# A decoder step on one core: the last down-projection tile by column halves, the final norm and outputs in two parts

## The reference

```
u = rmsnorm(h, mlp_norm[l]) @ w_up[l]             # 1024 -> 4096
h = h + square(relu(u)) @ w_down[l]               # 4096 -> 1024
...
y = rmsnorm(h, final_norm)                        # h * rsqrt(mean(h*h) + eps) * final_norm
```

## Time and profile before

| | |
|---|---|
| median of three runs | 1713.85 us (1711.11 to 1716.33) |
| the profiled execution | 1711.88 us, its span 1710.1 us |
| TensorE matmuls busy | 1603.4 us, 94% of the span |
| VectorE busy | 833.6 us, 49% |
| ScalarE busy | 562.3 us, 33% |
| DMA | 149.41 MB, mean 87 GB/s |

### The profile page before, as it was taken

How to read it: one execution, slowest core, us unless ns; L and a number is a source line. 1 busy time by engine, 2 the same in 40 slices (tenths; PEclk the granted TensorE clock), 3 DMA queues, 4 the chain that set the end, 5 groups by cost and what they waited for, 6 DMA issues and landing times.

```text
span 1710.1 us, 29033 instructions
## 1 busy us (share of the span) xinstructions
PE 1603.4 (94%) x11509; PEld 1481.6 (87%) x11509; DVE 833.6 (49%) x1227; ACT 562.3 (33%) x879; POOL 79.5 (5%) x93
## 2 busy tenths in 40 slices
PE   3889999878999999999989689999999999999998
PEld 3778999768999999999988456776799999999998
DVE  5845566654542433334576645655454334243343
ACT  4412222333331322323342115554333223132243
POOL 1720000001000000000000000000000000000000
PEclk8899999979999999999999889999999999999999
DMA  6433322203223222222233221543132322222221
GB/s 194 147 122 89 91 87 76 76 27 105 75 87 87 74 86 86 86 74 86 75 90 101 61 79 41 147 133 97 50 87 75 87 74 86 85 74 86 75 85 55
DMA packets 228795, 149.41 MB, mean 87 GB/s; under 512 B 11057, under 2 KB 222402, under 8 KB 228706
## 3 DMA queue, kind: packets, MB, share of 16 engines
q1 hardware_dynamic: 218802, 123.75, 25.2%
q0 software_dynamic: 6112, 20.54, 3.9%
q10 hardware_dynamic: 3792, 3.93, 0.7%
HBM read 140.52 MB, written 7.68 MB: 87 GB/s over the span
## 4 chain that ended last, share of the span: by engine, by line
PE 83%; DVE 11%; ACT 3%; issue 1%; DMA 1%; DVEq 0%; ACTq 0%; SPq 0%
PE ps L576 63%; PE ps L1050 3%; PE ps L1008 2%; DVE wl L1512 2%; PE ps L1077 2%; PE ps L991 1%; PE ps L918 1%; DVE ml L1516 1%; PE ps L953 1%; PE ps L954 1%; PE ps L704 1%; DVE ss L1522 1%; DVE t L1806 1%; PE ps L781 1%; ACT wh L1155 1%
## 5 line engine op out<-in xcount | busy, mean ns | idle before, releaser
L576 PE MATMUL ps<-xh,wh 128*128 128x288 f32 x1542 | 338.7, 302 | 2.2 <-DVE wl L1512 2.2
L576 PE MATMUL ps<-mh,wh 128*128 128x288 f32 (+1 forms) x1424 | 318.4, 300 | 17.9 <-DVE wl L1512 16.6
L576 PE MATMUL ps<-xh,wl 128*128 128x288 f32 x1542 | 331.6, 297 | 0.0
L576 PE MATMUL ps<-xl,wh 128*128 128x288 f32 x1542 | 331.5, 297 | 0.0
L576 PE MATMUL ps<-ml,wh 128*128 128x288 f32 (+1 forms) x1424 | 316.0, 298 | 0.0
L576 PE MATMUL ps<-mh,wl 128*128 128x288 f32 (+1 forms) x1424 | 315.9, 298 | 0.0
L1155 ACT ACTIVATE wh<-raw 128x1024 fp32r<-128x1024 f32 (+1 forms) x195 | 202.2, 1037 | 280.0 <-PE ps L576 262.1
L1512 DVE TENSOR_TENSOR wl<-raw,wh 128x1024 fp32r<-128x1024 f32 (+1 forms) x195 | 236.1, 1211 | 90.1 <-ACT wh L1155 88.7
L576 PEld LDWEIGHTS ps<-xh,wh 128*128 128x128 f32 x1542 | 250.6, 190 | 9.7 <-issue 5.3
L576 PEld LDWEIGHTS ps<-mh,wh 128*128 128x128 f32 x1424 | 236.8, 192 | 20.7 <-DVE wl L1512 17.2
L576 PEld LDWEIGHTS ps<-xl,wh 128*128 128x128 f32 x1542 | 250.1, 190 | 0.0
(11 more groups left out here) (296 smaller groups left out, 1440.9 us busy)
## 6 DMA issues: line engine op xcount, KB each, us to landing
raw<-in_w_up SPq DMA_DIRECT2D x64, 512.0 KB, 4.0
raw<-in_w_down SPq DMA_DIRECT2D x64, 512.0 KB, 3.6
pages<-in_cache_mla SPq DMA_DIRECT2D x128, 160.0 KB, 2.2
raw<-in_a_w_in SPq DMA_DIRECT2D x26, 512.0 KB, 4.0
memkc<-in_cache_mem_k POOLq DMA_DIRECT2D x16, 256.0 KB, 3.9
memvc<-in_cache_mem_v POOLq DMA_DIRECT2D x16, 256.0 KB, 4.5
raw<-in_a_w_out SPq DMA_DIRECT2D x8, 512.0 KB, 4.2
raw<-in_b_w_out SPq DMA_DIRECT2D x8, 512.0 KB, 4.7
```

What stands on the lines that cost most here:

```text
L576: last = mm(ps[:, 2 * (m % 2) + c, 0:n], w[:, s, kk, :], x(kk, col, n), start=(kk == 0 and nth == 0), stop=(kk == k - 1 and nth == 2))
```

## The change

The last down tile of each group is computed as two calls of `dense`, column half 0 first, half 1 behind it. Half 0 now counts on a new semaphore `left_ready`. For tile 194 alone the work behind it is done by halves too: VectorE adds 288 columns of the residual (`y_res`), ScalarE squares them (`y_sq`) and writes 288 columns of `ytmp`, VectorE adds 288 columns to `ss` (`y_ss`), first for half 0, then for half 1. This tile no longer counts on `acc_free` and `sq_used`.

The end runs in two parts: row blocks 0 and 1 (rows 0 to 255, within column half 0), then row blocks 2, 3 and the sample block. In each part come the sums, the roots, the reciprocals, the transposes and the scaled copies. The transposes use banks (n+4)%7 in place of n%7. Each row block leaves in two DMAs of 2 KB rows: SP sends features 0 to 511 when VectorE has them, and ScalarE itself issues the DMA for features 512 to 1023 behind its own copy.

```diff
+        left_ready, y_res, y_sq, y_ss, y_out_act = sem("left_ready"), sem("y_res"), sem("y_sq"), sem("y_ss"), sem("y_out_act")
...
                 sp.wait_ge(y_row_dve, n + 1)
-                sp.wait_ge(y_row_act, n + 1)
                 dst = o["y_p"][0, P * n:P * n + P, :] if n < RT else o["y_s"].rearrange("b t d -> (b t) d")
-                sp.dma_start(dst, yrow[n][0:P if n < RT else NS, :]).then_inc(y_out, 16)
+                sp.dma_start(dst[:, 0:512], yrow[n][0:P if n < RT else NS, 0:512]).then_inc(y_out, 16)
             sp.wait_ge(y_out, 16 * (RT + 1))
+            sp.wait_ge(y_out_act, 16 * (RT + 1))
...
-                if k - 1 in part and half != 0:
-                    last.then_inc(acc_ready, 1)
+                if k - 1 in part:
+                    last.then_inc(left_ready if half == 0 else acc_ready, 1)
...
-                    for j in range(KD):
+                    for j in range(KD - 1):
                         dense(m0 + base + GROUP + j, tiles(mh), tiles(ml), i=i, k=KD,
                               ready=(h_lo, lambda kk: at(h0 + base // 2 + kk + 1, i, GROUP)) if j == 0 else None)
+                    for half in range(2):
+                        dense(m0 + base + LAP - 1, tiles(mh), tiles(ml), i=i, k=KD, half=half)
...
+            for first, stop in ((0, 2), (2, RT + 1)):
+                pe.wait_ge(y_ss, 1 if first == 0 else 2)
+                if first:
+                    pe.wait_ge(y_rms, 1)
+                for r in range(first, stop):
+                    rows = P if r < RT else NS
+                    last = mm(ps[0:rows, 7, 64 * r:64 * r + 64], ss[:, P * r:P * r + rows], ones[:, 0:64], start=True, stop=True)
+                last.then_inc(ss_ps, 1)
+                pe.wait_ge(acc_free, M_END - 1)
+                pe.wait_ge(y_ready, KD if first == 0 else KD + 1)
+                for n in range(2 * first, 2 * stop):
+                    r, g = n // 2, n % 2
+                    rows = P if r < RT else NS
+                    if n >= 7:
+                        pe.wait_ge((y_row_dve, y_row_act)[(n - 7) % 2], (n - 7) // 2 + 1)
+                    for j in range(4):
+                        last = pe.transpose(ps[0:rows, (n + 4) % 7, P * j:P * j + P], ytmp[:, 4 * g + j, P * r:P * r + rows], ident[:, :])
+                    last.then_inc(y_tr, 1)
...
-                        if last:
+                        if last and m == M_END - 1:
+                            for c in range(2):
+                                part = slice(HALF * c, HALF * c + HALF)
+                                act.wait_ge(y_res, c + 1)
+                                if c == 0:
+                                    act.wait_ge(sq_used, C[sq_ready].n)
+                                do(f(sq[:, part], res[:, j, part], ACT.Square), C[y_sq])
+                                do(f(ytmp[:, j, part], res[:, j, part], ACT.Copy, scale=gain[:, G_FIN + j:G_FIN + j + 1]), C[y_ready])
+                        elif last:
...
+            for first, stop in ((0, 2), (2, RT + 1)):
+                act.wait_ge(ss_ps, 8 if first == 0 else 9)
+                full = min(stop, RT)
+                do(f(vec[:, 48 + first:48 + full], ps[:, 7, 64 * first:64 * full:64], ACT.Sqrt, bias=EPS, scale=1.0 / D), own if first else C[y_rms])
+                if first:
+                    do(f(vec[0:NS, 48 + RT:49 + RT], ps[0:NS, 7, 64 * RT:64 * RT + 1], ACT.Sqrt, bias=EPS, scale=1.0 / D), C[y_rms])
+                act.wait_ge(y_inv, 1 if first == 0 else 2)
+                for r in range(first, stop):
+                    rows = P if r < RT else NS
+                    act.wait_ge(y_tr, 2 * r + 2)
+                    do(f(yrow[r][0:rows, 512:D], ps[0:rows, (2 * r + 5) % 7, :], ACT.Copy, scale=vec[0:rows, 56 + r:57 + r]), C[y_row_act])
+                    dst = o["y_p"][0, P * r:P * r + P, 512:D] if r < RT else o["y_s"].rearrange("b t d -> (b t) d")[:, 512:D]
+                    act.dma_start(dst, yrow[r][0:rows, 512:D]).then_inc(y_out_act, 16)
...
+                        if last and m == M_END - 1:
+                            for c in range(2):
+                                dve.wait_ge(*((acc_ready, M_END) if c else (left_ready, 2 * NGROUP + 2)))
+                                part = slice(HALF * c, HALF * c + HALF)
+                                do(tt(res[:, j, part], res[:, j, part], ps[:, 2 * (m % 2) + c, 0:HALF], ALU.add), C[y_res])
+                                dve.wait_ge(y_sq, c + 1)
+                                do(tt(ss[:, part], ss[:, part], sq[:, part], ALU.add), C[y_ss])
+                            continue
```

More of the change, by code:

```diff
@@ L1145, in _ @@
                                        me_hi, ms_exp, ms_pt, ms_hi, r_act, r_os, r_osb, r_sq, r_std, r_hi, qa_hi,
-                                       kv_act, u_exp, u_pt, u_hi, l_keys_act, l_new, l_exp, l_alpha, uv_hi, y_ready, y_rms, y_row_act)}
+                                       kv_act, u_exp, u_pt, u_hi, l_keys_act, l_new, l_exp, l_alpha, uv_hi, y_ready, y_rms, y_row_act, y_sq)}
             f = act.activation
@@ L1503, in _ @@
                                        c_done, c_row, qa_lo, qr_ready, uk_T, kv_dve, l_q, u_max, u_norm, u_lo,
-                                       l_keys_dve, l_probs, l_back, l_max, l_o, l_fin, uv_lo, y_inv, y_row_dve)}
+                                       l_keys_dve, l_probs, l_back, l_max, l_o, l_fin, uv_lo, y_inv, y_row_dve, y_res, y_ss)}
             C[x_lo].n = KD
@@ L2026, in _ @@
             out_and_mlp(1, None)
[L2027 to L2033, removed]
+            for first, stop in ((0, 2), (2, RT + 1)):
+                dve.wait_ge(y_rms, 1 if first == 0 else 2)
+                full = min(stop, RT)
+                do(dve.reciprocal(vec[:, 56 + first:56 + full], vec[:, 48 + first:48 + full]), own if first else C[y_inv])
+                if first:
+                    do(dve.reciprocal(vec[0:NS, 56 + RT:57 + RT], vec[0:NS, 48 + RT:49 + RT]), C[y_inv])
+                for r in range(first, stop):
+                    rows = P if r < RT else NS
+                    dve.wait_ge(y_tr, 2 * r + 1)
+                    do(ts(yrow[r][0:rows, 0:512], ps[0:rows, (2 * r + 4) % 7, :], vec[0:rows, 56 + r:57 + r], None, ALU.mult), C[y_row_dve])
 def constants():
```

## The result

The changed kernel takes 1703.19 us on the median (1698.94 to 1704.74, 6 runs) and the kernel before 1714.05 (1709.96 to 1716.33, 6 runs); ratio 0.994, 95% interval 0.9921 to 0.9959. I had forecast 1710.7 (1706.5 to 1714.3), no change beyond 0.3%. It is faster by about 0.6%, three and a half times what I had worked out, and outside the range.

A forecast was written before the change was run, and what follows sets the result against it. TensorE's chain and, at the end, the backed-up output queue were taken to bound the kernel. Splitting at 0 and an end 3.1 us shorter took the median from 1713.85 to 1710.7 us, range 1706.5 to 1714.3.

The forecast's parts named there:

- The tail: From the last tile's end to the span's end: TensorE's idle stretch gone, outputs issued earlier; 3.1 us less.
- The chain ran over ScalarE: In the output part, ScalarE's copies, DMA issues (0.45 us each) and roots set the pace; last copy ends at 1703.7 us.
- the dip in the transfer: Output DMA slices at the end: two groups, with a dip near 1702 us between row blocks 1 and 2.
- the sum: End of the output transfer: sample block 1.2 us at half rate, landing at 1706.6 in place of 1709.7; 3.1 us less.
- Splitting the tiles: Eight down tiles run half by half: no instruction added, cost taken as 0, bounds 0 to under 0.1 us.
- The bounds of the range: Whole time: C with the spread among runs reaches down to 1706.5 us, A and most of B up to 1714.3.
- Rival D: Elsewhere in the kernel: another granted clock in a few stretches moves 1 to 4 us either way; chance 0.05.
- A: At the end, ScalarE's issues at 1.20 us choke it, leaving 0.1 to 1 us gain, 1713.3 us; chance 0.13.
- B: Output transfer: 2 KB packets cost 0.151 us each, so it lands 1.9 us later than before, 1715.8 us; chance 0.07.
- C: At the end, TensorE's earlier finish carries through with cheap issues and packets: gain 4 to 4.6 us, 1709.5 us; chance 0.13.
- TensorE's 4 us: Sums and transposes at the end: without the idle stretch they finish at 1701.0 us, 4 us earlier than 1705.05.
- The rule on issuing engines: Output DMAs: queues from several engines share the same 16 DMA engines, so a second queue saves only issue time, nothing in transfer.

The follow-up runs named there:

- one early flip per layer: Against the changed kernel: SP issues the outputs, only each layer's second up tile (43 and 132) and tile 194 computed half by half; 1701.9 us (10 runs).

## Why the prediction was wrong

*The tail: right.* Idle stretch of 2.53 us gone; clock 1.00 through the transposes, 0.11 us each; first scaled copy 1690.84, 2.2 us behind the last tile as forecast (1697.2 - 1695.06), first issue 2.95 us behind it (3.0 forecast). ScalarE's issues took 0.36 us, not 0.45, and the last copy ended 8.3 us behind the tile (8.6). A 2 KB packet took 0.087 us, the median of the trace (0.09 taken). 3.2 us measured, 3.1 forecast. The chain ran over ScalarE as said, and the dip in the transfer came where it was said. Two things flatter the match. The 3.2 us hold for this pair of traces, and at equal clock the end gained 2.1; that the trace of before had the low clock in its transposes was in my rows, that it need not be there was not. And the sum took 1.2 us for the sample block, where my own packet price, 128 packets at half rate, gives 1.44.

*Splitting the tiles: wrong, and this is the step that failed.* I took 0 from rows that show single halves at 0.1333 us and whole tiles at 0.1335, with bounds of 0 and +0.1 us. The half tiles do cost nothing: their own steps are 0.132 and 0.1335. What I did not ask is what they do to the tiles behind them. There they turn the pace of all that follow: 60 tiles at 6.24 us in place of 6.40, 9.9 us with the split tiles' own 0.04 each, and the splits alone took 9.4 us off the median. A gain was shut out by my bounds for no reason that the rows gave; I read a steady 0.1334 us as what such a matmul costs, though tile 131 of the trace that I had ran at 0.1300.

A page could have made me ask. The Trainium skill (TensorE: Matmul & The Clock Gate, section on 56 ns in place of 53.3) gives for matmuls in a row the columns over 2.4 GHz plus about 2.5 ns; for 288 columns that is an estimate of 122.5 ns. Neither pace in these traces reaches it, 130.0 and 133.4 ns, so the measurement decides here. The step has a weight load of its own, of which that figure says nothing. The 11 ns a matmul above it, some 67 us over the 128 feed-forward tiles, did not foretell a second pace, but they were a reason not to take the step for a fixed price.

*The bounds of the range* were made from terms of the end alone. Rival D named other stretches, but only by another granted clock, and gave it 0.05; the windows show the clock at 1.00 in both paces.

*Rivals A, B, C:* none. ScalarE's issues were shorter than taken, the packets went by bytes, and TensorE's 4 us did not carry through.

*The rule on issuing engines*, cited in the prediction from the Trainium skill (DMA: Bandwidth & Descriptors, section on issuing engines not being separate DMA queues), held, with more behind it than I drew from it. By it the second queue gives the transfer nothing, and the traces show that here it cost 0.4 us (11.97 against 11.57), as ScalarE had the copies to do.

What stays open: why a row of matmuls has two paces, and what sets the one at a layer's start. In the twelve profiled executions that run the first tiles of the feed-forward whole and in the ordinary order, all began layer 0's at 0.1334 and ten of the twelve layer 1's. Nor is it shown what made single runs of the kernel before take 1700.2 and 1705.9 us. Nothing here shows which resource holds the 3.4 ns.

## What to carry to other kernels

A loop that runs without a gap at full clock need not be at its floor; here it was 2.6% above a pace that the same matmuls can hold. An edit of the order inside it has no safe price of nothing, and its bounds must hold a gain and a loss for every tile that follows, not for the edited ones alone. Look at windows of equal length and count instructions; the busy share was the same for both paces. At an end that is bound by writing out, start the first transfer early; keeping the issue off the engine that makes the data brought 0.4 us here, and not cutting the rows 0.3.

## What the runs showed of the hardware

- For 288-column matmuls with a weight load each, alternating between two PSUM banks, at a granted clock of 1.00: two steady paces, 0.1334 us (steps of 131, 131, 132, 140 ns) and 0.1300 us (128, 132). A pace held for over 2000 matmuls (tiles 58 to 105 of the kernel with one split per layer).
- 48 matmuls in the order 24 and 24 turned it over each time it was settled, in both directions (0.1334 to 0.1300 and back), 41 times in nine traces; two such tiles cancel. A single swap and a mirrored order at the tile's border did not move the longer pace; the one border that met the shorter pace ended it.
- The pace after a wait differs between traces of the same code: layer 1's tile 132 started at 0.1300 in two of twelve and at 0.1334 in ten, and within one trace tiles 131 and 132, with a wait between them, had different paces. Of 10 runs of one kernel with one early flip per layer one took 1688.2 us, six 1700.3 to 1702.2, three 1707.9 to 1710.5; the groups are 13 and 8 us apart, where one layer's 62 tiles by 0.16 are 10, so the paces of the layers are likely most of it; only one of the ten was profiled, and this is not shown. With a flip in every group each execution spends half its tiles at either pace, whichever it starts with: 1698.9 to 1704.7 us in all eleven runs of the changed kernel. A comparison of few runs can mislead: one run of before took 1700.2.
- After 2.54 us of idle TensorE the granted clock stayed at 1.00 through the sums and transposes in two of seven traces with the old end (14.07 us) and was at 0.50 for part of them in five (15.22 to 16.36 us).
- Output packets of 2 KB from SBUF took 0.087 us and those of 4 KB 0.160 (medians; means 0.093 and 0.175); the 64-row sample block, whose transfer is the last in all traces, runs at about 160 to 270 GB/s, the 128-row ones at about 380 to 400.
- A DMA's issue of 128 rows took 0.36 us on ScalarE and 0.34 on SP in the changed kernel, that of 64 rows 0.53 and 0.57; ten in close order on SP took 0.33 to 0.67 each.
